# HGRN, second four heads: decay factors over three places, differences two levels ahead, one low part and the far scores elsewhere in the order

## The chip, the cores and the metric

The kernel runs on one core of one Trainium2 chip. The metric is device time in microseconds (us), lower is better. Times are shown for three runs of the kernel before, and for one profiled execution, whose trace gives every row below. In all of it, 256 tokens go through two transformer blocks; the change is in one sublayer, the HGRN mixer, sublayer 6 of 0 to 7.

## The reference, cut to what matters

The reference runs a first block (sparse attention with a convolution, then SwiGLU) and a second block of two layers (SwiGLU, differential attention, SwiGLU; then SwiGLU, HGRN, SwiGLU). The HGRN mixer is:

```python
def hgrn2(h, w_in, w_o, out_gain, lb):
    q, f, i, g = jnp.split(h @ w_in, [F, 2 * F, 2 * F + D_MODEL], axis=-1)
    log_forget = jnp.logaddexp(jnp.log(lb32), jnp.log1p(-lb32) + jax.nn.log_sigmoid(f32))
    k = (1.0 - lb32) * jax.nn.sigmoid(-f32)
    def step(state, inp):                    # chunks of 64 tokens
        G = jnp.cumsum(gc, axis=2)
        o_inter = jnp.einsum('bhtk,bhkv->bhtv', qc * jnp.exp(G), state)
        decay = jnp.exp(jnp.where(causal, G[:, :, :, None, :] - G[:, :, None, :, :], -jnp.inf))
        scores = jnp.einsum('bhtk,bhsk,bhtsk->bhts', qc, kc, decay)
        o_intra = jnp.einsum('bhts,bhsv->bhtv', scores, vc)
        ...
    o = rms_norm(o, out_gain.reshape(H, dv)) * jax.nn.silu(g)
    return o.reshape(B, S, D_MODEL) @ w_o
```

There are 8 heads with keys and values of 128, D_MODEL = 1024, S = 256. All is float32.

## The kernel before, in words

**Weights.** Every weight matrix streams through a ring of three slots in units of 128 x 2048 numbers. Sync's queue loads a unit (`raw`), ScalarE (ACT) rounds it to a high part (`hi(unit)`, whi, line 663), VectorE (DVE) takes the rest (`lo(unit)`, wlo, line 1250), and TensorE (PE) multiplies with both (three matmuls for one product, line 2062). The load of a unit waits for the low part of the unit three before it. In HGRN the units are U to U+19: U to U+15 for the input projection, U+16 to U+19 for the output product (`output_product`, called with `beside`, which puts other PE work between its parts). The output product goes over the units for the first 128 tokens, then for the others.

**The order** of all work is written out by hand, one list of calls for each engine; engines meet by semaphores only. On one engine nothing passes what stands ahead of it.

**HGRN on heads.** The heads are handled in two halves of four. For each half the scores of 256 tokens are made without the recurrence: level 0 is k times q on the diagonal, level L from 1 to 7 takes the pairs whose tokens lie in two neighbouring blocks of 64, 32, ... 1 tokens, level 8 the pairs between the first and the second 128 tokens, the "far" scores. For a half and a level:

- `differences(half, level)` (DVE, lines 1907 and 1909, for level 8 lines 1913 to 1916): G relative to the middle of each block pair, into a place that `decayed(level, half)` names.
- `exps(half, level)` (ACT, line 968, for level 8 lines 970 to 972): its exponential, in place.
- `decay(half, level)` (DVE, lines 1925 and 1928): times k and q, in place.
- `scores(half, level)` (PE, line 2507): 16 matmuls (8 for level 8) into bank 6 or 7 of PSUM by the level's parity; it waits for the decay and for the mask copy of the level before.
- `take_scores(half, level)` (DVE, lines 1937 and 1943): a masked copy of the product into the scores.

`step(half, level)` on DVE is the decay of a level, the differences of the next level, and the masked copy of the level before. `decayed` gives odd levels a place in `hf` and even levels one in `xn`, each with one half for heads 0 to 3 and one for heads 4 to 7. The differences of a level overwrite the place of two levels before, so from level 3 on they wait for the scores of that level (semaphore `lv_mm`, one count for each call of `scores`, nine for a half).

**Behind the levels** of the second half: `values(1, 0)` and `values(1, 1)` on PE (lines 2520 and 2522) multiply scores and values for the two token tiles, the second also with the far scores, which ACT copies (`take_far_scores(1)`, line 978). ACT squares the products (`square_last`, line 1017), DVE sums them (`sum_last`, lines 1964 and 1966) and multiplies product and gate (line 1969), GpSimd (POOL) takes the root (line 486), DVE scales (`norm_last`, line 1975), PE transposes (`turn_heads`, line 2177), DVE multiplies with the gain (`take_mixed`, line 1981), and ACT and DVE split it into high and low parts (lines 683 and 1303). Unit U+18's matmuls for the first tokens wait for that. ACT does the gate's silu (`silu_of(1)`, line 994) between `exps(1, 8)` and the squares. On PE `sum_columns(7)` (line 2070, 32 operations), the modulation sums for the next sublayer, stands between `values(1, 1)` and the turns.

Of the kernel before, what the change touches and what calls it, by code (L numbers as in the profile page):

```python
# [32 lines left out]
NT = TOK // P  # L33
# [25 lines left out]
LEVELS = (64, 32, 16, 8, 4, 2, 1)  # L59
# [90 lines left out]
def two_blocks(  # L150
# [30 lines left out]
    with ExitStack() as ctx:  # L181
        def sb(name, shape, dt=F32):
            return ctx.enter_context(nc.sbuf_tensor(name, shape, dt))

        def sem(name):
            return ctx.enter_context(nc.semaphore(name))
# [8 lines left out]
        xn = sb("xn", [P, NT, D])  # L195
        hf = sb("hf", [P, KT, TOK])
# [19 lines left out]
        half = st[:, 240:241]  # L216
# [25 lines left out]
        def by_head(flat):  # L242
            return flat.rearrange("p (h n) -> p h n", h=HEADS)
# [8 lines left out]
        def of_half(place, half):  # L252

            return place[:, HALF * half:HALF * (half + 1), :]

        def decayed(level, half):

            return of_half(hf if level % 2 else by_head(xn[:, :, :].rearrange("p t n -> p (t n)")), half)

        def halves(place, level):  # L260

# [62 lines left out]
        lv_mm, lv_copy, g_silu = sem("lv_mm"), sem("lv_copy"), sem("g_silu")  # L324
# [329 lines left out]
        def _(sc):  # L654
# [268 lines left out]
            def hgrn():  # L923

                U = FIRST[6]
# [49 lines left out]
                def take_far_scores(half):  # L975

                    sc.wait_ge(lv_mm, (len(LEVELS) + 2) * (half + 1))
                    sc.activation(far_scores(half), ps[:, 6, :].rearrange("p (h n) -> p h n", h=HALF), ACT.Copy).then_inc(lv_far, 1)
# [11 lines left out]
                def silu_of(half):  # L990

                    g = h_g[:, :, half * BANK:(half + 1) * BANK]
                    sc.wait_ge(vg_out, 6 + 2 * half)
                    sc.activation(g, g, ACT.Silu).then_inc(g_silu, 1)
# [19 lines left out]
                def square_last(t):  # L1014

                    sc.wait_ge(pv_mm, 4 + t + 1)
                    sc.activation(hf[:, HALF + 2 * t:HALF + 2 * t + 2, :], bank(h_bank(1, t)).rearrange("p (h n) -> p h n", h=2),
                                  ACT.Square).then_inc(head_sq, 1)
# [64 lines left out]
                exps(1, 7)  # L1083
                exps(1, 8)
                silu_of(1)
                square_last(0)
                take_far_scores(1)
                square_last(1)
                mixed_of(1, 0)
                mixed_of(1, 1)  # L1090
# [4 lines left out]
            for row, src in ((0, c), (8, c_2), (16, b_ada[0:1, 0:2 * D])):  # L1095
                n = src.shape[-1] // P
# [7 lines left out]
            U = FIRST[0]  # L1104
# [130 lines left out]
        def _(ve):  # L1235
# [10 lines left out]
            def lo(unit, lap=0, n=UNIT):  # L1246

                slot = unit % RING
                ve.wait_ge(w_hi, used(unit, lap))
                ve.tensor_tensor(wlo[:, slot, 0:n], raw[:, slot, 0:n], whi[:, slot, 0:n].bitcast(F32), ALU.subtract)\  # L1250
                    .then_inc(w_lo, 1)
# [249 lines left out]
            U = FIRST[0]  # L1501
# [355 lines left out]
            def hgrn():  # L1857

                U = FIRST[6]
# [36 lines left out]
                def differences(half, level):  # L1896

                    E, G = decayed(level, half), of_half(h_G, half)
                    if level >= 3:
                        ve.wait_ge(lv_mm, (len(LEVELS) + 2) * half + level - 1)  # L1900
                    if level == 1:
                        ve.wait_ge(k_ready, half + 1)
                    if level <= len(LEVELS):
                        n = LEVELS[level - 1]
                        e, g = halves(E, level), halves(G, level)
                        middle = g[:, :, 0, n - 1:n].to_broadcast((P, HALF * TOK // (2 * n), n))
                        done = ve.tensor_tensor(e[:, :, 0, :], middle, g[:, :, 0, :], ALU.subtract)
                        if level > 1:
                            done = ve.tensor_tensor(e[:, :, 1, :], g[:, :, 1, :], middle, ALU.subtract)
                    else:  # L1910
                        e, g = (a.rearrange("p h (c n) -> p h c n", n=CHUNK) for a in (E, G))
                        total = [g[:, :, c, CHUNK - 1:CHUNK].to_broadcast((P, HALF, CHUNK)) for c in range(3)]
                        link(ve.tensor_tensor(e[:, :, 0, :], total[0], g[:, :, 0, :], ALU.subtract))
                        ve.tensor_tensor(e[:, :, 0, :], e[:, :, 0, :], total[1], ALU.add)
                        ve.tensor_tensor(e[:, :, 1, :], total[1], g[:, :, 1, :], ALU.subtract)
                        done = ve.tensor_tensor(e[:, :, 3, :], g[:, :, 3, :], total[2], ALU.add)
                    done.then_inc(lv_sub, 1)
# [28 lines left out]
                def step(half, level):  # L1946

                    decay(half, level)
                    if level <= len(LEVELS):
                        differences(half, level + 1)  # L1950
                    take_scores(half, level - 1)

                def gate_heads(t):
# [6 lines left out]
                def sum_last(t):  # L1960

                    ve.wait_ge(head_sq, 6 + t + 1)
                    sums = st[:, 124 + 8 * t:128 + 8 * t]
                    link(ve.tensor_reduce(sums, hf[:, HALF + 2 * t:HALF + 2 * t + 2, :].rearrange("p a (h d) -> p (a h) d", h=2),
                                          axis=AX.X, op=ALU.add))
                    ve.tensor_scalar(sums, sums, 1.0 / P, EPS2, ALU.mult, ALU.add).then_inc(block_mean, 1)
                    if t == 0:
                        ve.wait_ge(g_silu, 2)
                    link(ve.tensor_tensor(h_o[:, 1, t, :], bank(h_bank(1, t)), h_g[:, t, BANK:D], ALU.mult))
# [45 lines left out]
                lo(U + 14)  # L2015
                differences(1, 1)
                step(0, 8)
                step(1, 1)
                lo(U + 15)
                step(1, 2)  # L2020
# [9 lines left out]
                lo(U + 17)  # L2030
                step(1, 5)
                step(1, 6)
                lo(U + 18)
                step(1, 7)
                step(1, 8)
                for t in range(NT):
                    sum_last(t)
                for t in range(NT):
                    norm_last(t)
                for t in range(NT):  # L2040
# [16 lines left out]
        def _(pe):  # L2057
# [407 lines left out]
            def hgrn():  # L2465

                U = FIRST[6]
# [13 lines left out]
                def scores(half, level):  # L2481

                    if level == 0:
                        pe.wait_ge(f_exp, half + 1)
                        pe.wait_ge(q_copied, half + 1)
                        if half:
                            pe.wait_ge(lv_copy, len(LEVELS) + 1)
                            pe.wait_ge(lv_far, 1)
                        else:
                            pe.wait_ge(gate_set, 7)  # L2490
                    else:
                        pe.wait_ge(lv_mul, (len(LEVELS) + 1) * half + level)
                        pe.wait_ge(lv_copy, (len(LEVELS) + 1) * half + max(level - 1, 1))
                    k, q, E = of_half(h_k, half), of_half(h_q, half), decayed(level, half)
                    for t in range(NT if level <= len(LEVELS) else 1):
                        cols = slice(t * P, (t + 1) * P)
                        for h in range(HALF):
                            dst = ps[:, 6 + t, h * P:(h + 1) * P]
                            if level == 0:
                                lhsT, rhs = k[:, h, cols], q[:, h, cols]  # L2500
                            elif level <= len(LEVELS):
                                g, n = t * HALF + h, LEVELS[level - 1]
                                lhsT, rhs = E[:, h, cols], later(E[:, h:h + 1, cols], level)[:, 0, :, :]
                                dst = level_bank(level)[:, g * P // 2:(g + 1) * P // 2].rearrange("p (b n) -> p b n", n=n)
                            else:
                                lhsT, rhs = E[:, h, 0:P], E[:, h, P:TOK]
                            done = pe.matmul(dst, lhsT, rhs, start=True, stop=True)  # L2507
                    done.then_inc(lv_mm, 1)
# [72 lines left out]
                def beside(j, t):  # L2581

                    if (j, t) == (0, 1):
                        scores(1, 4)
                    elif (j, t) == (1, 0):
                        scores(1, 5)
                    elif (j, t) == (2, 0):
                        scores(1, 6)
                        scores(1, 7)
                        values(1, 0)  # L2590
                        scores(1, 8)
                        values(1, 1)
                        sum_columns(7)
                        turn_heads(1, 0)
                        turn_heads(1, 1)
# [33 lines left out]
            U = FIRST[0]  # L2629
# [157 lines left out]
```

## Time and profile before

| | us |
|---|---|
| median of three runs | 1488.42 |
| lowest, highest | 1486.87, 1488.79 |
| profiled execution, its own time | 1488.98 |
| its span (first to last instruction) | 1487.30 |
| PE busy, DVE busy, ACT busy | 1409.5, 1060.7, 693.5 |
| mean granted clock of PE | 0.966 |

The granted clock is a share of full speed. Busy time counts an engine's own operations; in the timelines an operation's length is from its start to its end, and one behind it can start a little before that end. The bracket at the end of a row is the idle time ahead of it and what ended it. The HGRN stage's second half of heads lies at about 1209 to 1274 us of the span.

### The profile page before, as it was taken

The page shows a single profiled execution, that of the slowest core. Times are in us where ns is not written, and L with a number is a line of the kernel's source. Part 1 is how long each engine was busy: PE and PEld are TensorE (multiplying, and loading weights), DVE is VectorE, ACT ScalarE, POOL GpSimd, SP SyncE. Part 2 cuts the span into 40 slices and gives each one's busy share as a digit, 9 for nine tenths or more (in the row PEclk, how much of TensorE's full clock was granted, in tenths as well). Part 3 has the DMA queues.
Part 4 walks back from the last instruction along what each step waited for, and adds up shares of the span by engine and source line. Part 5 has one row for each costly group of instructions (what it writes and reads, how often), then busy time and mean ns, then how long its engine had stood idle before and what let it go on. Part 6 is the DMA issues. An engine that isn't in the chain of part 4 may idle for free.

```text
span 1487.3 us, 19356 instructions
## 1 busy us (share of the span) xinstructions
PE 1409.5 (95%) x6922; PEld 1176.2 (79%) x6922; DVE 1060.7 (71%) x1127; ACT 693.5 (47%) x897; POOL 186.2 (13%) x279
## 2 busy tenths in 40 slices
PE   5997899999799999999999999999999998899998
PEld 5896688888588887767788887888888987788887
DVE  5788877776678877685667775688866878655555
ACT  2463354433444345665643435444447764543442
POOL 3103211110301110221101102011101010000000
PEclk9995999999799999999999999999999998899999
DMA  9835379995389994533589973899945342256661
GB/s 355 301 143 212 129 260 313 309 315 186 129 279 345 373 378 146 187 113 114 169 274 312 309 270 108 296 337 343 349 142 170 114 142 85 95 188 214 229 226 66
DMA packets 187525, 335.61 MB, mean 226 GB/s; under 512 B 9169, under 2 KB 123453, under 8 KB 187216
## 3 DMA queue, kind: packets, MB, share of 16 engines
q1 hardware_dynamic: 160528, 237.95, 47.4%
q0 software_dynamic: 26736, 96.71, 18.1%
q8 instruction: 34, 0.56, 0.1%
q10 hardware_dynamic: 208, 0.23, 0.0%
q14 instruction: 19, 0.16, 0.0%
HBM read 332.23 MB, written 2.63 MB: 225 GB/s over the span
## 4 chain that ended last, share of the span: by engine, by line
PE 82%; DVE 8%; ACT 4%; POOL 2%; issue 2%; DMA 1%; SPq 0%; DVEq 0%; ACTq 0%; POOLq 0%
PE ps L2062 72%; DVE wlo L1250 2%; POOL st L486 2%; PE ps L2177 1%; PE ps L2246 1%; PE ps L2070 1%; PE ps L2507 1%; ACT whi L663 1%; DMA big<-in_w_ada 1%; ACT hf L671 1%; PE ps L2605 1%; ACT xn L696 1%; DVE xn L1312 1%; ACT xn L703 0%; PE ps L2191 0%
## 5 line engine op out<-in xcount | busy, mean ns | idle before, releaser
L1250 DVE TENSOR_TENSOR wlo<-raw,whi 128x2048 fp32r<-128x2048 f32 x206 | 470.2, 2285 | 151.5 <-ACT whi L663 150.4
L2062 PE MATMUL ps<-whi,hhi 128*128 128x512 f32 (+1 forms) x1208 | 494.9, 410 | 15.7 <-DVE hlo L1298 8.9
L663 ACT ACTIVATE whi<-raw 128x2048 fp32r<-128x2048 f32 x215 | 409.7, 1909 | 209.0 <-PE ps L2062 165.1
L2062 PE MATMUL ps<-whi,hlo 128*128 128x512 f32 (+1 forms) x1208 | 478.7, 396 | 0.0
L2062 PE MATMUL ps<-wlo,hhi 128*128 128x512 f32 (+1 forms) x1208 | 478.2, 396 | 0.0
L2062 PEld LDWEIGHTS ps<-whi,hhi 128*128 128x128 f32 x1208 | 232.3, 192 | 67.6 <-issue 11.9
L2062 PEld LDWEIGHTS ps<-whi,hlo 128*128 128x128 f32 x1208 | 231.6, 192 | 50.2
L2062 PEld LDWEIGHTS ps<-wlo,hhi 128*128 128x128 f32 x1208 | 232.5, 192 | 46.0 <-issue 1.9
L2062 PE MATMUL ps<-whi,ahi 128*128 128x512 f32 x400 | 156.1, 390 | 0.0
L2062 PE MATMUL ps<-whi,alo 128*128 128x512 f32 x400 | 155.7, 389 | 0.0
L2062 PE MATMUL ps<-wlo,ahi 128*128 128x512 f32 x400 | 155.7, 389 | 0.0
L1265 DVE SCALAR_TENSOR_TENSOR ada_acc<-ada_raw,csil,ada_acc 128x1024 f32<-128x1024 f32 x104 | 130.2, 1278 | 0.0
L519 POOL DMA_DIRECT2D ada_raw<-in_ada_w x96 | 50.9, 530 | 545.4 <-DVE ada_acc L1265 533.7
L747 ACT ACTIVATE act<-ps 128x256 f32<-128x256 f32 x110 | 41.9, 383 | 161.1 <-PE ps L2062 161.0
L751 ACT ACTIVATE ahi<-ps 128x512 fp32r<-128x512 f32 x50 | 29.9, 599 | 180.5 <-PE ps L2246 180.5
L1432 DVE TENSOR_TENSOR alo<-ps,ahi 128x512 fp32r<-128x512 f32 x50 | 34.5, 690 | 86.9 <-ACT ahi L751 86.9
L2062 PEld LDWEIGHTS ps<-whi,alo 128*128 128x128 f32 x400 | 75.1, 188 | 15.6
L2062 PEld LDWEIGHTS ps<-wlo,ahi 128*128 128x128 f32 x400 | 75.1, 188 | 15.4
L2062 PEld LDWEIGHTS ps<-whi,ahi 128*128 128x128 f32 x400 | 75.1, 188 | 15.4
L1427 DVE TENSOR_TENSOR act<-act,ps 128x256 f32<-128x256 f32 x110 | 42.9, 416 | 42.7 <-ACT act L747 42.6
L486 POOL TENSOR_TENSOR st<-st 128x1 f32<-128x1 f32 (+3 forms) x35 | 45.8, 1310 | 169.2 <-DVE st L1336 69.6
L2062 PE MATMUL ps<-hhi,whi 128*128 128x256 f32 x224 | 64.4, 287 | 1.2 <-DVE wlo L1250 1.2
(284 smaller groups left out, 1445.6 us busy)
## 6 DMA issues: line engine op xcount, KB each, us to landing
raw<-in_ffn_w_in SPq DMA_DIRECT2D x176, 512.0 KB
ada_raw<-in_ada_w POOLq DMA_DIRECT2D x96, 512.0 KB, 5.2
raw<-in_ffn_w_down SPq DMA_DIRECT2D x44, 1024.0 KB
big<-in_ada_w POOLq DMA_DIRECT2D x48, 512.0 KB, 6.2
raw<-in_hgrn_w_in SPq DMA_DIRECT2D x16, 1024.0 KB
raw<-in_attn_w_qkv SPq DMA_DIRECT2D x12, 1024.0 KB
ada_raw<-in_w_ada POOLq DMA_DIRECT2D x23, 512.0 KB, 4.9
raw<-in_w_gate SPq DMA_DIRECT2D x22, 512.0 KB
```

The costliest lines, as they stand in the source:

```text
L486: pool.tensor_tensor(cols, cols, half.to_broadcast((P, width)), ALU.pow).then_inc(signal, 1)
L519: pool.dma_start(ada_slot(p), w[bass.ds(kt * P, P), first + j * D:first + (j + 1) * D])\
L663: sc.activation(whi[:, slot, 0:n], raw[:, slot, 0:n], ACT.Copy).then_inc(w_hi, 1)
L671: done = sc.activation(hf[:, kt, toks], ps[:, 2 * t + 1, (kt - 4) * P:(kt - 3) * P], ACT.Identity, scale=modc[:, s % 2, 8 + kt:9 + kt], bi ...
L696: sc.activation(xn[:, t, cols], xs[:, t, cols], ACT.Square, scale=1.0 / 32, accum_out=st[:, part:part + 1]).then_inc(sums_s, 1)
L747: sc.activation(act[:, t, :], ps[:, 4 + t, 0:FC], ACT.Silu).then_inc(silu_done, 1)
L751: sc.activation(ahi.rearrange("p k n -> p (k n)"), bank(6), ACT.Copy).then_inc(ahi_ready, 1)
L1250: ve.tensor_tensor(wlo[:, slot, 0:n], raw[:, slot, 0:n], whi[:, slot, 0:n].bitcast(F32), ALU.subtract)\
L1265: ve.scalar_tensor_tensor(acc, ada_slot(p), csil[:, bass.ds((0 if a < 2 else 8) + kt, 1)], acc, ALU.mult, ALU.add).then_inc(a_used, 1)
L1427: ve.tensor_tensor(act[:, t, :], act[:, t, :], ps[:, 4 + t, FC:2 * FC], ALU.mult).then_inc(act_ready, 1)
L1432: ve.tensor_tensor(a_lo, bank(6), a_hi.bitcast(F32), ALU.subtract).then_inc(alo_ready, 1)
L2062: done = pe.matmul(dst, lhsT, rhs, start=first and n == 0, stop=final and n == 2, skip_group_check=True)
```

## The change

Three places instead of two hold the decay factors of the second half of heads: levels 1, 4, 7 in `hf`, heads 4 to 7; levels 2, 5, 8 in `xn`, heads 4 to 7; levels 3, 6 in `xn`, heads 0 to 3, which the first half of heads has left by then. On DVE, `step(1, level)` makes the differences of two levels ahead instead of one, up to level 8, and `differences(1, 2)` stands by itself after `step(0, 8)`. The waits follow: the differences of level 4 and on wait for the scores three levels before, those of level 3 for the last scores of the first half.

On DVE, `lo(U + 18)` goes from between `step(1, 6)` and `step(1, 7)` to between `sum_last(0)` and `sum_last(1)`. On PE, `scores(1, 8)` goes ahead of `values(1, 0)`. On ACT, `take_far_scores(1)` goes ahead of `square_last(0)`.

```diff
@@ -255,7 +255,12 @@
 
         def decayed(level, half):
 
-            return of_half(hf if level % 2 else by_head(xn[:, :, :].rearrange("p t n -> p (t n)")), half)
+            wide = by_head(xn[:, :, :].rearrange("p t n -> p (t n)"))
+            if half == 0:
+                return of_half(hf if level % 2 else wide, 0)
+            if level % 3 == 0:
+                return of_half(wide, 0)
+            return of_half(hf if level % 3 == 1 else wide, 1)
 
         def halves(place, level):
 
@@ -1083,8 +1088,8 @@
                 exps(1, 7)
                 exps(1, 8)
                 silu_of(1)
+                take_far_scores(1)
                 square_last(0)
-                take_far_scores(1)
                 square_last(1)
                 mixed_of(1, 0)
                 mixed_of(1, 1)
@@ -1896,8 +1901,10 @@
                 def differences(half, level):
 
                     E, G = decayed(level, half), of_half(h_G, half)
-                    if level >= 3:
-                        ve.wait_ge(lv_mm, (len(LEVELS) + 2) * half + level - 1)
+                    if level >= 3 + half:
+                        ve.wait_ge(lv_mm, (len(LEVELS) + 2) * half + level - 1 - half)
+                    if half and level == 3:
+                        ve.wait_ge(lv_mm, len(LEVELS) + 2)
                     if level == 1:
                         ve.wait_ge(k_ready, half + 1)
                     if level <= len(LEVELS):
@@ -1946,8 +1953,8 @@
                 def step(half, level):
 
                     decay(half, level)
-                    if level <= len(LEVELS):
-                        differences(half, level + 1)
+                    if level <= len(LEVELS) - half:
+                        differences(half, level + 1 + half)
                     take_scores(half, level - 1)
 
                 def gate_heads(t):
@@ -2015,6 +2022,7 @@
                 lo(U + 14)
                 differences(1, 1)
                 step(0, 8)
+                differences(1, 2)
                 step(1, 1)
                 lo(U + 15)
                 step(1, 2)
@@ -2030,11 +2038,11 @@
                 lo(U + 17)
                 step(1, 5)
                 step(1, 6)
-                lo(U + 18)
                 step(1, 7)
                 step(1, 8)
-                for t in range(NT):
-                    sum_last(t)
+                sum_last(0)
+                lo(U + 18)
+                sum_last(1)
                 for t in range(NT):
                     norm_last(t)
                 for t in range(NT):
@@ -2587,8 +2595,8 @@
                     elif (j, t) == (2, 0):
                         scores(1, 6)
                         scores(1, 7)
+                        scores(1, 8)
                         values(1, 0)
-                        scores(1, 8)
                         values(1, 1)
                         sum_columns(7)
                         turn_heads(1, 0)
```

## Rows read from the trace of the kernel before

**Rows 1.** The page: busy time, share of the span, instructions of PE; the chain by engine.

```profile
PE 1409.5 (95%) x6922; PEld 1176.2 (79%) x6922; DVE 1060.7 (71%) x1127; ACT 693.5 (47%) x897; POOL 186.2 (13%) x279
...
PE 82%; DVE 8%; ACT 4%; POOL 2%; issue 2%; DMA 1%; SPq 0%; DVEq 0%; ACTq 0%; POOLq 0%
```

**Rows 2.** The chain of waits, 1190 to 1320 us: start, us, engine, tile, line.

```profile
1258.35 2.07 PE ps L2520 x8
...
1266.60 3.83 PE ps L2070 x32
...
1273.30 14.51 PE ps L2062 x54
```

**Rows 3.** Timeline of VectorE (DVE), 1195 to 1330 us: start, us, then idle before.

```profile
1214.38 0.69 DVE L1925 TENSOR_TENSOR hf<-hf,big 128x512 f32<-128x512 f32 x1 [2.44 <-ACT hf L966]
...
1224.34 0.69 DVE L1925 TENSOR_TENSOR xn<-xn,big 128x512 f32<-128x512 f32 x1 [2.66 <-ACT xn L968]
...
1246.51 0.69 DVE L1925 TENSOR_TENSOR xn<-xn,big 128x512 f32<-128x512 f32 x1 [0.49 <-ACT xn L968]
...
1249.52 2.29 DVE L1250 TENSOR_TENSOR wlo<-raw,whi 128x2048 fp32r<-128x2048 f32 x1
1251.72 0.69 DVE L1925 TENSOR_TENSOR hf<-hf,big 128x512 f32<-128x512 f32 x1
...
1252.93 0.42 DVE L1913 TENSOR_TENSOR xn<-big 128x256 f32<-128x256 f32 x1
...
1254.40 1.30 DVE L1943 COPY_PREDICATED ada_acc<-mask,ps 128x512 f32<-128x512 uint8 x1
...
1257.00 1.29 DVE L1943 COPY_PREDICATED ada_acc<-mask,ps 128x512 f32<-128x512 uint8 x1
1261.09 0.69 DVE L1964 TENSOR_REDUCE st<-hf 128x4 f32<-128x512 f32 x1 [2.79 <-ACT hf L1017]
...
1267.34 0.69 DVE L1964 TENSOR_REDUCE st<-hf 128x4 f32<-128x512 f32 x1 [4.77 <-ACT hf L1017]
...
1268.85 1.29 DVE L1975 TENSOR_TENSOR big<-big,st 128x512 f32<-128x512 f32 x2
1271.10 0.69 DVE L1981 TENSOR_TENSOR hf<-ps,vec 128x512 f32<-128x512 f32 x1 [0.95 <-PE ps L2177]
...
1275.14 2.29 DVE L1250 TENSOR_TENSOR wlo<-raw,whi 128x2048 fp32r<-128x2048 f32 x1 [1.11 <-ACT whi L663]
```

**Rows 4.** Timeline of TensorE (PE), the same stretch.

```profile
1212.51 1.05 PE L2507 MATMUL ps<-xn 128*128 128x128 f32 x8
...
1217.92 1.28 PE L2520 MATMUL ps<-big,ada_acc 128*128 128x128 f32 x10
...
1244.23 2.00 PE L2507 MATMUL ps<-hf 128*128 128x64 f32 x16 [0.41 <-DVE hf L1928]
...
1248.87 1.89 PE L2507 MATMUL ps<-xn 128*128 128x64 f32 x16
1253.07 3.25 PE L2507 MATMUL ps<-hf 128*128 128x64 f32 x16 [2.30 <-DVE hf L1928]
```

**Rows 5.** Timeline of ScalarE (ACT), the same stretch.

```profile
1240.20 1.06 ACT L968 ACTIVATE hf<-hf 128x1024 f32<-128x1024 f32 x1 [0.76 <-DVE hf L1909]
...
1257.07 1.06 ACT L994 ACTIVATE big<-big 128x1024 f32<-128x1024 f32 x1
...
1273.21 1.89 ACT L663 ACTIVATE whi<-raw 128x2048 fp32r<-128x2048 f32 x1
```

**Rows 6.** Windows of 2 us: engines' busy time, then PE's granted clock, DMA share, GB/s.

```profile
1254.00:1256.00 2.00, 2.00 (x11) 2.00 (x10) 1.91 (x4) 1.47 (x4) 0.00 (x0) 0.50 1.00 327
...
1276.00:1278.00 2.00, 2.00 (x7) 1.61 (x6) 1.43 (x1) 0.00 (x0) 0.00 (x0) 0.63 0.00 0
```

**Rows 7.** Timeline of GpSimd (POOL), 610 to 621 us and 1252 to 1312 us.

```profile
610.90 3.61 POOL L486 TENSOR_TENSOR st<-st 128x8 f32<-128x8 f32 x1 [3.83 <-DVE st L1733]
...
1268.31 1.01 POOL L486 TENSOR_TENSOR st<-st 128x4 f32<-128x4 f32 x1 [5.24 <-DVE st L1966]
```

## The prediction

> **What bounds the kernel now.** I read the page first, then the chain of waits around the edited stage, then the three engines' timelines there, and last the granted clock. The page says TensorE (PE) is busy for 95% of the span and carries 82% of the chain that ends last [rows 1]; over the whole kernel PE is the bound, so an edit off PE pays only where PE stands idle waiting for it, or runs at the lower clock. The chain shows such a place: from 1258.35 us it goes through `values(1, 0)`, then the column sums (3.83 us), and reaches the first matmul of unit U+18 only at 1273.30 [rows 2]. Before that PE is late on VectorE (DVE): it idles 0.41 us ahead of `scores(1, 5)` and 2.30 us ahead of `scores(1, 7)`, each ended by the decay product [rows 4]. DVE is back to back over the same stretch except for 0.49 us [rows 3]. So from about 1246 to 1258 DVE's queue is the bound, after that a chain that goes PE, ACT, DVE, PE; while it runs PE's clock is granted at 0.50 (1.2 GHz), and it is back at full (2.4 GHz) only near 1277 [rows 6]. Every microsecond by which U+18 starts earlier should show at the end, as everything behind it (rest of the output product, last SwiGLU) is ordered by PE.
>
> **Part 1: order of differences, and the third place.** No instruction is added; the same differences are issued one step earlier, and the places let them. `differences(1, 2)` now stands after `step(0, 8)`. DVE idles 2.44 us there, ended by ACT's exponential of level 1 at 1214.38 [rows 3]; one pair costs 1.21 us (a pair of equal shape: from 1251.72 to 1252.93), so it is free: cover 2.44, need 1.21. If that cover were gone it costs 1.2 us, yet another 2.66 us idle stands at 1224.34 behind ACT, which would take it up [rows 3]. `step(1, 1)` now makes level 3 in the place half 0 had in xn; it waits for `scores(0, 8)`, whose 8 matmuls run from 1212.51 to 1213.56 [rows 4], before DVE gets there at 1215.6: no wait. From 1224.34 on each step still issues one pair, until the last: `step(1, 6)` makes level 8 instead of 7, and `step(1, 7)` none. The pair saved before the last mask copy is 1.2 us. The exponential of level 6 no longer follows its own differences: ACT waited 0.76 us for level 5 at 1240.20 [rows 5]; now levels 5 and 6 (1.06 each) can follow the 17th high part and end near 1241.5. So the 0.49 us idle at 1246.51 [rows 3] goes: DVE starts `decay(1, 6)` at 1246.0. New waits: level 8 waits for `scores(1, 5)`, which end at 1246.2 [rows 4], while DVE is there at 1247.2: nothing. Were it late, the exponential of level 8 and three DVE operations would queue behind it.
>
> **Part 2: lo(U+18) moved behind sum_last(0).** One operation of 2.20 us (1249.52 to 1251.72 [rows 3]) leaves the queue ahead of `decay(1, 7)`. Walk the queue: `decay(1, 6)` 1246.0 to 1247.2, differences of level 8 (four operations, 1252.93 to 1254.40, 1.47 us [rows 3]) to 1248.7, mask copy 0.6 to 1249.3, `decay(1, 7)` to 1250.5. Late next is PE: `scores(1, 6)` start at 1248.87 behind U+17's first token tile, whose start does not move (`decay(1, 5)` keeps its time), and end at 1250.8 [rows 4]; the mask copy of level 6 starts at 1250.9, 1.3 us, then `decay(1, 8)` 1.2, then the copy of level 7, 1.3 [rows 3]: end 1254.7 against 1258.3. ACT's exponential of level 8 is done near 1250, earlier than its decay. Gain here 3.6 us.
>
> **Part 3: scores(1, 8) ahead of values(1, 0), far scores ahead of the square.** The 8 matmuls of level 8 run from the end of `decay(1, 8)`, 1253.4, to 1254.5 at 1.05 us [rows 4], under the last mask copy. silu_of(1) (a table load, then 1.06 us [rows 5]) now ends near 1252.4, so ACT copies the far scores at once, by 1255.1, while `values(1, 0)` runs (1254.75 to 1255.8, ten such matmuls taking 1.28, or 0.11 from start to start [rows 4]). `values(1, 1)` follows with no wait: 16 more, to 1257.6. On DVE: 0.65 from the values' end to the first reduction (1260.42 to 1261.09 [rows 2, 3]) makes 1256.45, `sum_last(0)` takes 1.5 (as 1267.34 to 1268.85), and then lo(U+18), 2.2, is on the path now: 1260.15. Only then `sum_last(1)`, ready since 1258.3. It starts at 1260.15 against 1267.34 [rows 3].
>
> **The tail.** Before, from `sum_last(1)` to U+18's start it was 5.96 us, of which PE's column sums held the first turn until 1270.4 [rows 2]. Now these sums (at most 3.83) run 1257.6 to 1261.4 and hold nothing. `norm_last(0)` is done 2.2 us after `sum_last(1)` starts (it begins 1.51 after, 0.65 long [rows 3]), four transposes at the lower clock take 0.8, and from take_mixed to U+18 it was 2.20 (1271.10 to 1273.30): 5.2 us. U+18 starts at 1265.35, against 1273.30: 7.95 us earlier. Then nothing differs: U+18 has its low part (1260.15), and lo(U+19) was 1.8 us behind U+18's start (1275.14, ended by the high part that begins at 1273.21 [rows 3, 5]) and stays so; U+19's first tile starts 4.7 us behind U+18 while the clock is low for 3.9 us, as before. The load of U+21 is issued 8 us later but its high part is read only about 18 us on.
>
> At that point a rule bears on the new neighbours: GpSimd's root of sum 0 now runs beside lo(U+18). The trace has a root beside such a low part that took 3.61 us, against 1.01 beside the multiplications by roots, which themselves start with no idle time (1268.85) while the root of 1268.31 runs [rows 3, 7]. So a stretch of the root ends with lo(U+18) plus 1.0, 1261.15, and `norm_last(0)` is due at 1261.65: hidden. The Trainium skill (SBUF — State Buffer, Who interferes with whom) says that a VectorE operation with both inputs in SBUF and a GpSimd operation exclude each other, and whichever starts first holds the port. By it the root, first here (1257.4 to 1258.4), would hold lo(U+18) back some 0.6 us, and the gain would be 7.4, not 7.95; the multiplication at 1268.85 speaks against that.
>
> **Sum.** 3.6 (to the last mask copy) + 3.6 (from there to `sum_last(1)`, 9.05 us down to 5.45) + 0.75 (tail) = 7.95. The profiled execution took 1488.98 (span 1487.30): 1481.0 for it. It lies 0.56 above the median of the three runs, so I forecast 1480.5.
>
> **Rivals.**
> A: the clock falls among the last scores already, as in the execution shown (half at 1254 [rows 6]). For it: PE still waits 0.6 us ahead of `scores(1, 8)` and 0.25 after. Against: there it idled 2.30 us first. Price: `values(1, 0)` 1.9, `values(1, 1)` 3.6, column sums 3.9, all PE's, make 1254.7 into 1264.1, and the turn to U+18 is 3.0: 1267.1, gain 6.2, time 1482.2.
> B: the clock never falls, or is back when U+18 starts: 12 matmuls then end 1.9 us sooner, but lo(U+19) is ready only 4.1 us after U+18's start, so 0.6 more: gain 8.6, time 1479.8. Against: after the column sums PE idles about 1 us, and about 1.5 again after the turns.
> C: the places don't let the differences run ahead, because a score that they wait for is later than I read; then only lo(U+18) and the score order act. Without the saved pair and the 0.49 us, minus the 0.4 that PE's `scores(1, 6)` would have taken: gain 6.7, time 1481.7.
> D, the other side: PE's gaps, now shorter but more, leave it at half clock from about 1254 through the whole output product. A unit's first 12 matmuls cost 5.1 us at the low spacing (0.43) and 2.7 at the full one; three tiles of the first token and three of the second are 14 us more, less the 3.9 us low clock that were paid before (1.9 us), against the 8 gained (6.2 with A): 1494. It decides from the fifth of the six tiles at half clock on (8 + 1.9 over 2.4 us each). Against: at 1277 the clock came back within 4 us of dense matmuls [rows 6], and nothing thins them now.
> E: a stage behind has a bound of its own (a load, a bias), and takes the gain: 1487 to 1488.4. Against: PE's 54 matmuls in one piece from 1273.30 [rows 2].
>
> **How the numbers follow.** Chances: forecast 0.62, A 0.15, B 0.08, C 0.07, D 0.03, E 0.05. The range 1478.4 to 1484.0 takes in the forecast, A, B and C, with the spread of the runs (1.9 us) on either side of B and A. 0.2% (3 us) is about what measurement tells from no change: faster 0.92 (forecast, A, B, C), same 0.05, slower 0.03.
>
> **What would show it.** Right: no low part between `decay(1, 6)` and the last mask copy, which ends near 1254.7; `scores(1, 8)` before `values(1, 0)`; lo(U+18) between the two reductions; U+18's first matmul near 1265. Wrong: DVE idle ahead of a difference (C), a half clock at 1254 (A), values waiting for the far copy, lo(U+18) held back by a root, or U+19's first matmul waiting on its low part (B).

## The result, and the profile after

The changed kernel takes 1480.88 us (median of 9 runs, 1477.95 to 1486.58) against 1488.42 (9 runs, 1485.45 to 1489.90): ratio 0.995, 95% interval 0.9937 to 0.9963. So it is about 0.5% faster, and the interval excludes no change. The forecast was 1480.5, and the time lies in its range.

The profiled execution took 1478.56 with a span of 1476.9, 10.4 us less than the one before. Not all of that is the change. The start of `decay(1, 2)`, ahead of which all is the same in both kernels but one pair of differences in an idle gap, is 3.76 us earlier, 1220.58 against 1224.34 [rows 3]. So I count from that point:

| us from the start of decay(1, 2) | before | before, second trace | changed | changed, second trace |
|---|---|---|---|---|
| last mask copy ends | 33.9 | 33.9 | 30.1 | 30.1 |
| `sum_last(1)` starts | 43.0 | 41.2 | 37.0 | 36.9 |
| first matmul of U+18 | 49.0 | 46.6 | 42.65 | 42.3 |
| end of the span | 263.0 | 260.7 | 256.3 | 256.1 |

A count such as x8 is of recorded instructions. A float32 matmul of the code leaves two of them (5 fillers of a run below give x10), so a level's x16 is 8 matmuls and the x8 of level 8 is 4; the texts ahead call them 16 and 8.

Line numbers are 5 to 8 higher in the changed kernel (L1925 is L1932, L1943 is L1950, L2520 is L2528, L2070 is L2078, L2062 is L2070). On the page, PE is as busy a share of a shorter span, 10.6 us less busy time than in [rows 1]:

```profile
PE 1398.9 (95%) x6922; PEld 1166.8 (79%) x6922; DVE 1059.8 (72%) x1127; ACT 693.3 (47%) x897; POOL 185.5 (13%) x279
```

VectorE's timeline of the changed kernel, which answers to [rows 3]:

```profile
1220.58 0.69 DVE L1932 TENSOR_TENSOR xn<-xn,big 128x512 f32<-128x512 f32 x1 [2.67 <-ACT xn L973]
...
1242.14 0.69 DVE L1932 TENSOR_TENSOR xn<-xn,big 128x512 f32<-128x512 f32 x1
...
1247.07 1.32 DVE L1950 COPY_PREDICATED ada_acc<-mask,ps 128x512 f32<-128x512 uint8 x1 [0.37 <-PE ps L2515]
...
1249.41 1.29 DVE L1950 COPY_PREDICATED ada_acc<-mask,ps 128x512 f32<-128x512 uint8 x1
1253.90 0.69 DVE L1971 TENSOR_REDUCE st<-hf 128x4 f32<-128x512 f32 x1 [3.20 <-ACT hf L1022]
...
1255.41 2.29 DVE L1255 TENSOR_TENSOR wlo<-raw,whi 128x2048 fp32r<-128x2048 f32 x1
1257.62 0.68 DVE L1971 TENSOR_REDUCE st<-hf 128x4 f32<-128x512 f32 x1
...
1261.03 0.69 DVE L1988 TENSOR_TENSOR hf<-ps,vec 128x512 f32<-128x512 f32 x1 [0.61 <-PE ps L2185]
...
1265.07 2.29 DVE L1255 TENSOR_TENSOR wlo<-raw,whi 128x2048 fp32r<-128x2048 f32 x1 [1.11 <-ACT whi L668]
```

`decay(1, 6)` starts 21.56 us after `decay(1, 2)`, with no idle time ahead, against 22.17 before; there is no low part between it and the last mask copy; the copy of level 6 (1247.07) waits 0.37 us for PE's scores. The copy at 1249.41 is the last. Then DVE idles 3.20 us to the first sum, does lo(U+18) at 1255.41, and starts the second sum right behind it with no idle time: the low part is what it waits behind.

TensorE's timeline of the changed kernel, which answers to [rows 4]:

```profile
1246.87 1.95 PE L2515 MATMUL ps<-hf 128*128 128x64 f32 x16
1249.55 2.00 PE L2515 MATMUL ps<-xn 128*128 128x128 f32 x8 [0.73 <-DVE xn L1935]
1251.34 2.11 PE L2528 MATMUL ps<-big,ada_acc 128*128 128x128 f32 x10
...
1254.85 3.63 PE L2078 MATMUL ps<-ones,ada_acc 128*128 128x1 f32 x32
1259.88 1.97 PE L2185 MATMUL ps<-kc,big 128*128 128x128 f32 x8 [1.39 <-DVE big L1982]
1263.23 0.79 PE L2070 MATMUL ps<-whi,hhi 128*128 128x512 f32 x1 [1.38 <-DVE hlo L1308]
```

The 2.30 us idle ahead of `scores(1, 7)` is gone (1246.87, no bracket); 0.73 us stands ahead of `scores(1, 8)`, now before the values. But the 8 instructions of level 8 take 2.00 us, not 1.05, and the first ten of the values 2.11, not 1.28: half clock. The windows of 2 us (engines' busy time, granted clock, DMA share, GB/s) say when:

```profile
1250.00:1252.00 2.00, 2.00 (x12) 2.00 (x11) 0.70 (x1) 0.41 (x1) 0.00 (x0) 0.50 0.00 0
...
1256.00:1258.00 2.00, 2.00 (x20) 2.00 (x20) 2.00 (x2) 0.00 (x0) 0.00 (x0) 1.00 0.00 0
...
1264.00:1266.00 2.00, 2.00 (x7) 1.51 (x6) 0.93 (x1) 1.04 (x1) 0.00 (x0) 0.50 0.00 0
```

It is at 0.50 at 1250, at full at 1256, and at 0.50 again when U+18 starts. The kernel before has such a return too, and I had not read it: my prediction has the clock at half from 1254 until near 1277. Its window from 1268 to 1270 is at 1.00, under the column sums, most of which ran at full clock:

```profile
1266.39 4.03 PE L2070 MATMUL ps<-ones,ada_acc 128*128 128x1 f32 x32
```

```profile
1268.00:1270.00 2.00, 2.00 (x20) 2.00 (x19) 1.93 (x5) 0.00 (x0) 1.01 (x1) 1.00 0.00 0
```

ScalarE's rows, which answer to [rows 5], show the far copy (L983) ahead of both squares (L1022), and the silu long done:

```profile
1247.49 1.06 ACT L999 ACTIVATE big<-big 128x1024 f32<-128x1024 f32 x1
1251.59 0.60 ACT L983 ACTIVATE ada_acc<-ps 128x512 f32<-128x512 f32 x1 [3.04 <-PE ps L2515]
1253.27 0.60 ACT L1022 ACTIVATE hf<-ps 128x512 f32<-128x512 f32 x1 [1.08 <-PE ps L2528]
```

GpSimd's root of the first sum, beside lo(U+18):

```profile
1254.87 1.01 POOL L491 TENSOR_TENSOR st<-st 128x4 f32<-128x4 f32 x1 [34.41 <-DVE st L1973]
```

### The profile page after: what moved, and what is told of

Same layout as the page of the kernel before. It is cut to its first block, busy times and chain, and to the rows that moved or that the text cites. A ratio compares the mean times of both kernels' runs of the same rounds, so it can differ in the third digit from the quotient of the medians.

```text
span 1476.9 us, 19356 instructions
## 1 busy us (share of the span) xinstructions
PE 1398.9 (95%) x6922; PEld 1166.8 (79%) x6922; DVE 1059.8 (72%) x1127; ACT 693.3 (47%) x897; POOL 185.5 (13%) x279
## 4 chain that ended last, share of the span: by engine, by line
PE 78%; DVE 9%; ACT 5%; DMA 3%; issue 2%; POOL 2%; SPq 0%; DVEq 0%; ACTq 0%; POOLq 0%
PE ps L2070 69%; DVE wlo L1255 2%; DMA raw<-in_ffn_w_in 2%; PE ps L2185 2%; ACT whi L668 2%; POOL st L491 2%; PE ps L2515 1%; PE ps L2254 1%; PE ps L2078 1%; DMA big<-in_w_ada 1%; ACT hf L676 1%; ACT xn L701 1%; PE ps L2613 1%; DVE xn L1317 1%; ACT xn L708 0%
## 5 line engine op out<-in xcount | busy, mean ns | idle before, releaser
L2070 PE MATMUL ps<-whi,hhi 128*128 128x512 f32 (+1 forms) x1208 | 493.5, 409 | 16.6 <-DVE hlo L1303 8.9
L2070 PE MATMUL ps<-whi,hlo 128*128 128x512 f32 (+1 forms) x1208 | 477.3, 395 | 0.0
L2070 PE MATMUL ps<-wlo,hhi 128*128 128x512 f32 (+1 forms) x1208 | 476.2, 394 | 0.0
L2070 PEld LDWEIGHTS ps<-whi,hhi 128*128 128x128 f32 x1208 | 231.5, 192 | 68.2 <-issue 11.9
L2070 PEld LDWEIGHTS ps<-whi,hlo 128*128 128x128 f32 x1208 | 230.3, 191 | 50.0
L2070 PEld LDWEIGHTS ps<-wlo,hhi 128*128 128x128 f32 x1208 | 231.7, 192 | 45.7 <-issue 1.9
L2070 PE MATMUL ps<-whi,ahi 128*128 128x512 f32 x400 | 156.1, 390 | 0.0
L2070 PE MATMUL ps<-whi,alo 128*128 128x512 f32 x400 | 155.7, 389 | 0.0
L2070 PE MATMUL ps<-wlo,ahi 128*128 128x512 f32 x400 | 155.6, 389 | 0.0
L2070 PEld LDWEIGHTS ps<-whi,alo 128*128 128x128 f32 x400 | 75.1, 188 | 15.6
L2070 PEld LDWEIGHTS ps<-whi,ahi 128*128 128x128 f32 x400 | 75.1, 188 | 15.6 <-issue 0.2
L2070 PEld LDWEIGHTS ps<-wlo,ahi 128*128 128x128 f32 x400 | 75.1, 188 | 15.4
L1432 DVE TENSOR_TENSOR act<-act,ps 128x256 f32<-128x256 f32 x110 | 42.8, 415 | 41.8 <-ACT act L752 41.7
L2070 PE MATMUL ps<-hhi,whi 128*128 128x256 f32 x224 | 64.3, 287 | 1.2 <-DVE wlo L1255 1.2
```

The source lines that it names most:

```text
L1432: ve.tensor_tensor(act[:, t, :], act[:, t, :], ps[:, 4 + t, FC:2 * FC], ALU.mult).then_inc(act_ready, 1)
L2070: done = pe.matmul(dst, lhsT, rhs, start=first and n == 0, stop=final and n == 2, skip_group_check=True)
```

## The experiments

Lengths are from the start of `decay(1, 2)`, as in the table; "copy" is the end of the last mask copy. Every time is a median with the ratio to the kernel before, run beside it.

**The change taken apart.** First the differences alone: `decayed`, the waits, `step` and `differences(1, 2)` as in the change, nothing else.

> The kernel before with part 1 alone: three places and differences two levels ahead, differences(1, 2) after step(0, 8); lo(U+18) and the scores stay. I measure the stage from the start of decay(1, 2) on VectorE to the first matmul of U+18: 48.96 us before, 42.65 in the changed kernel. Theory (VectorE's queue): one pair of differences (1.2 us) and the wait of 0.49 for the exponential of level 6 leave the queue, so the stage is 1.7 to 1.9 shorter, 47.2; time about 1486.6. Rival (a score waited for is late and takes the place of the pair): 49.0, time 1488.4.

Measured: copy 31.8 (2.1 sooner), second sum 40.9, yet U+18 at 49.95; 1485.26 us, ratio 0.9965 (0.9952 to 0.9978). The queue's gain is there and the rival falls, but in this one trace it was lost on PE, after the second sum. Its column sums:

```profile
1266.26 6.83 PE L2078 MATMUL ps<-ones,ada_acc 128*128 128x1 f32 x32
```

The same 32 instructions took 4.03 before and 3.63 in the changed kernel. In this run the clock fell at 1257.1 and stayed at half for 23.9 us. To the end of the span it is 262.6, against 263.0 and 260.7 before: this one trace shows no gain at its end, the times do.

Then lo(U+18) alone:

```diff
-                lo(U + 18)
                 step(1, 7)
                 step(1, 8)
-                for t in range(NT):
-                    sum_last(t)
+                sum_last(0)
+                lo(U + 18)
+                sum_last(1)
```

> The kernel before with lo(U+18) alone moved between sum_last(0) and sum_last(1). Theory: 2.2 us leave the queue ahead of decay(1, 7), PE's scores(1, 6) give little of it back (level 8's differences wait for them), so the last mask copy ends about 2.1 us sooner; in its new place lo(U+18) is hidden, as the second sum is 9 us behind the copy there: stage 46.9, time about 1486.3. Rival (it only changes places on the path and costs its 2.2 us behind the first sum): 49.0, time 1488.4.

Measured: copy 32.4, U+18 47.4, end 261.1; 1483.81 us, ratio 0.9967 (0.9949 to 0.9984). The copy came 1.6 us sooner, not 2.1. U+18 stands between the two traces of before (49.0 and 46.6), so the stage does not decide between the theory and the rival; the times show a gain of 0.33%.

Then the far scores alone, `scores(1, 8)` ahead of `values(1, 0)` and the far copy ahead of the square:

> The kernel before with the order of level 8 alone changed: scores(1, 8) ahead of values(1, 0) on PE, the far copy ahead of the square on ScalarE. From decay(1, 2) on VectorE, the last mask copy still ends at 33.9 us. Theory (PE and ScalarE work leaves the chain behind that copy: level 8's matmuls 1.9 and the far copy 0.7 at half clock): stage 46 to 47 where the column sums meet the full clock, 3 us more where they meet half of it (the run of differences alone had 6.83 us for them against 3.63 to 4.03 elsewhere). Rival (the far scores were hidden anyway): 49.

Measured: copy 34.0, second sum 38.9, U+18 44.3, end 257.3; 1485.52 us, ratio 0.9971 (0.9953 to 0.999). More than the theory said, as PE came back to the full clock among the values:

```profile
1254.55 2.08 PE L2507 MATMUL ps<-xn 128*128 128x128 f32 x8 [0.72 <-DVE xn L1928]
1256.42 1.90 PE L2520 MATMUL ps<-big,ada_acc 128*128 128x128 f32 x10
...
1259.72 3.63 PE L2070 MATMUL ps<-ones,ada_acc 128*128 128x1 f32 x32
```

Level 8's 8 instructions take 2.08 us (half clock), the column sums 3.63 (full). In the trace this part alone gives 4.6 us at U+18 against the first trace of before, and 2.3 against the second.

The three parts alone gain 0.35, 0.33 and 0.29% in their times. Together that is 0.97%, more than the 0.5% of the whole change (0.64% in its second group of runs), so they hardly add up as if each were independent of the others. The three are not told apart by their times.

Parts 1 and 3 without part 2, lo(U+18) in its old place:

> The changed kernel with lo(U+18) back between step(1, 6) and step(1, 7), so parts 1 and 3 without part 2. Theory (in its new place between the two sums lo(U+18) gives back on the path what it saved in the queue): the last mask copy ends at 31.8 us instead of 30.1, but the second sum starts at about 35.5 instead of 37.0, and U+18 at 40.7 to 42.5 by the clock, no later than the 42.3 and 42.65 of the changed kernel. Rival (my prediction's sum, where part 2 is worth its 2.2 in the queue): about 44.5.

Measured: copy 31.85, second sum 36.9, U+18 42.4, end 255.3; 1482.0 us, ratio 0.9959 (0.9939 to 0.998). U+18 starts where it starts in the changed kernel (42.65, 42.3). So between the two sums the low part gives back what it saved in the queue: the copy is 1.7 us later without part 2, the second sum no later. It was not the 35.5 that I expected: level 8 and the first ten instructions of the values ran at half clock here too (2.08 and 2.04 us). The times (1482.0, and 1481.17 for the changed kernel in another group of runs) don't separate the two.

**The changed kernel and the kernel before once more.**

> The changed kernel once more. Theory: the profiled pair differs by 10.4 us of span, of which 3.8 stood before anything changed (opening, before 127 us), so that part does not repeat; the stage again takes 42 to 43.5 us, by where TensorE's clock falls, and the time is 1479 to 1483. Rival (the 3.8 us belong to the change): the first root of GpSimd again at 123.5 us and not near 127, time 1478.

> The kernel before once more, for its second trace. I measure also from the start of decay(1, 2) on VectorE to the end of the span: 263.0 us before, 256.3 and 256.1 in the two traces of the changed kernel. Theory (that length is the kernel's own, the rest of the 10.4 us between the first two traces came from ahead of the stage): 262 to 265 by where the clock falls, last mask copy again at 33.9. Rival (before varies there by as much as the gain): under 260.

The changed kernel again: 1481.17 us, ratio 0.9936 (0.9914 to 0.9957), the stage 42.3. Its first root came at 123.25, which by itself fits the rival; but the kernel before has 127.16 in one trace and 122.95 in the other, so the opening moves without the change. The end, 256.1 against 256.3, repeats. Over all traces of this study `decay(1, 2)` started between 1220.6 and 1227.1. The kernel before again: 1490.55, ratio to itself 1.0015 (0.9998 to 1.0032), which is about what the times resolve. Its length to the end is 260.7, below the 262 I expected: in the first trace `values(1, 1)` ran at half clock, in the second at full, with the column sums at 3.63.

```profile
1259.37 2.08 PE L2520 MATMUL ps<-big,ada_acc 128*128 128x128 f32 x8 [3.27 <-DVE ada_acc L1943]
...
1265.64 3.63 PE L2070 MATMUL ps<-ones,ada_acc 128*128 128x1 f32 x32
```

So the first trace's 9.05 us from the last copy to the second sum were 7.2 in the second. The far scores and the values were behind idle times of PE in both: 2.3 us ahead of `scores(1, 7)`, and ahead of the values 2.03 in the first trace, 3.27 in the second.

**lo(U+18) ahead of both sums.** In the changed kernel:

```diff
+                lo(U + 18)
                 sum_last(0)
-                lo(U + 18)
                 sum_last(1)
```

> The changed kernel with lo(U+18) ahead of sum_last(0) instead of behind it. Theory: VectorE idles 3.2 us there (1250.7 to 1253.9 in the changed kernel's trace), which covers 2.2; sum_last(1) then starts when its square is done, 1.9 us sooner, and the turns are held by the column sums, so U+18 starts 1.4 us sooner: stage 41.3, time 1.4 below the changed kernel, 1479.5. Rival (lo(U+18) is hidden where it stands, the tail is PE's own chain of values and column sums): stage unchanged at 42.6, same time.

> The changed kernel with lo(U+18) ahead of both sums, once more, beside the run with filled gaps. Theory: last mask copy at 30.1, second sum at 33.9 if the values run at full clock and up to 2.8 later at half; U+18 at 39.3 with the column sums at full clock, up to 5 us later where they meet the half clock. Rival (the first look's 39.3 is the queue's own figure and has no clock in it): 39.3 again whatever the clock.

Measured, first trace: second sum 33.9, U+18 39.3, end 252.1; 1479.39 us, ratio 0.993 (0.9909 to 0.9952). Second trace: 35.2, 40.6, 253.6; 1478.11, ratio 0.9932 (0.9907 to 0.9957). Both are shorter than the changed kernel's 256.1 and 256.3. The first gave more than the 1.4 us expected since its values ran at full clock; the second ran them at half and has 1.3 us more, so the rival (39.3 whatever the clock) falls. The second trace compares with the changed kernel at the same clock: its second sum is 1.8 to 1.9 us earlier and U+18 1.7 to 2.0. The times don't separate the two kernels: 1479.39 and 1481.17 in one group of runs, with intervals that overlap. VectorE in the first trace: the low part right behind the copy, then the sums, the second one waiting 0.24 us for its square.

```profile
1255.44 2.32 DVE L1255 TENSOR_TENSOR wlo<-raw,whi 128x2048 fp32r<-128x2048 f32 x1
1257.68 0.67 DVE L1971 TENSOR_REDUCE st<-hf 128x4 f32<-128x512 f32 x1
...
1259.38 0.69 DVE L1971 TENSOR_REDUCE st<-hf 128x4 f32<-128x512 f32 x1 [0.24 <-ACT hf L1022]
```

And PE there, level 8 in 1.16 us, the values' first ten in 1.38:

```profile
1254.49 1.16 PE L2515 MATMUL ps<-xn 128*128 128x128 f32 x8 [0.73 <-DVE xn L1935]
1255.70 1.38 PE L2528 MATMUL ps<-big,ada_acc 128*128 128x128 f32 x10
...
1264.84 0.79 PE L2070 MATMUL ps<-whi,hhi 128*128 128x512 f32 x1 [1.80 <-DVE hlo L1308]
```

**Without running ahead.** That kernel with the differences one level ahead in two places:

> The kernel with lo(U+18) ahead of both sums and the far scores first, but the differences one level ahead in two places, as before the change (parts 2 and 3 without part 1). Theory (the queue of VectorE sets the last mask copy): the copy ends at 32.4 as in the run of the low part alone, 2.2 later than the 30.1 with part 1; U+18 2.2 us later, 41.5 to 42.8; 254.5 to 256 us from decay(1, 2) to the end against 252.1 and 253.6. Rival (differences ahead are hidden once the low part is gone): 30.1 to 31 for the copy, and the same end.

Measured: copy 32.4, U+18 45.1, end 259.2; 1484.53 us, ratio 0.9968 (0.9953 to 0.9983). The copy is where the theory has it and the rival falls, but U+18 is 4.5 to 5.8 us later, not 2.2, and the end is beyond the 254.5 to 256 that I gave. `scores(1, 8)` have 2.07 us of idle ahead. The clock was at half from before them into the values, and it fell again within the column sums (4.81 us):

```profile
1254.39 2.08 PE L2507 MATMUL ps<-xn 128*128 128x128 f32 x8 [2.07 <-DVE xn L1928]
...
1260.30 4.81 PE L2070 MATMUL ps<-ones,ada_acc 128*128 128x1 f32 x32
```

**The clock itself.** PE's gaps filled, and ScalarE's high part of U+19 moved up:

```diff
+                        fill(4, 5)
                         scores(1, 8)
                         ...
                         turn_heads(1, 1)
+                        fill(5, 12)
```

`fill(b, n)` is n matmuls of the identity by ones into bank b, which nothing reads.

> As the kernel with lo(U+18) ahead of both sums, and PE's idle gaps filled with matmuls of the identity by ones into free banks: 5 ahead of scores(1, 8), 12 ahead of U+18; nothing reads them. Theory (the half clock comes from thin PE work there, and costs 1 to 5 us by where it falls): the clock stays at full through the values, the last mask copy at 30.1, U+18 at 39.3 to 40, its first 12 matmuls in 2.8 us instead of 4 to 5; time equal to the unfilled kernel or up to 1.5 us less. Rival (the single-column sums alone bring the clock down, whatever fills the gaps): the clock still falls within 5 us behind the column sums, and the time is the same or 0.5 us more, for the fillers.

> The kernel with lo(U+18) ahead of both sums, and ScalarE's hi(U+19) ahead of the far copy, where ScalarE idles 2.2 to 3.0 us (the high part takes 1.9). Theory: lo(U+19) starts 1.0 us sooner, but U+19's first matmul waits for it only where U+18's tile runs at full clock from its start, which no trace of the stage shows unless its gap is filled; so the stage and the time stay, at most 0.6 less. Rival (the high part comes into the way of the far copy or the square): U+18 up to 0.5 us later.

> The kernel with lo(U+18) ahead of both sums, hi(U+19) ahead of the far copy, 5 filling matmuls ahead of scores(1, 8) and 6 (not 12) ahead of U+18. With 12 they ran 1.6 us past the data, and took from the clock all of the stage's 10.2 us of half clock but 3.4. Theory (what is left of the clock's cost in the tail is U+18's tile at half clock, 2 us): U+18 at 39.3 to 39.7, its 12 first matmuls in 2.7 to 4 us, and 250.5 to 252 us from decay(1, 2) to the end against 252.1, 252.1 and 253.6 unfilled. Rival (6 are too few to bring the clock back before U+18): as unfilled, 252.1 to 253.6.

With 12 fillers: 1477.19 us, ratio 0.9917 (0.9893 to 0.9942); the values at full clock, half clock only for 3.4 us. It did fall within the column sums all the same, as the rival had it. And the fillers ran past their gap and U+18 started at 41.6, so my 39.3 to 40 was missed; end 253.5. The time is not told apart from the 1478.11 of the unfilled kernel beside it. hi(U+19) early alone: 1479.11 (0.9902 to 0.9958), lo(U+19) 1.2 us sooner, U+18 39.3 and end 252.1 as in the first trace without it: worth nothing there, as expected. Both, with 6 fillers ahead of U+18: 1475.41 us, ratio 0.9912 (0.9891 to 0.9933), U+18 40.3 (0.6 later than I said), its 12 first matmuls in 2.85 us, end 250.8, the least of all. PE of this kernel: fillers, level 8, fillers, U+18.

```profile
1254.31 1.33 PE L2592 MATMUL ps<-ones,kc 128*128 128x128 f32 x10
1255.48 1.06 PE L2515 MATMUL ps<-xn 128*128 128x128 f32 x8
...
1264.76 1.99 PE L2592 MATMUL ps<-ones,kc 128*128 128x128 f32 x12
1266.51 0.48 PE L2070 MATMUL ps<-whi,hhi 128*128 128x512 f32 x1
```

This version is faster than the kernel before. That it is faster than the changed kernel too is likely and not shown: its interval just fails to touch the first one of the changed kernel (0.9937 to 0.9963) and overlaps the second (0.9914 to 0.9957), and it has four runs, in a group of its own on another chip.

## Why the prediction was right, step by step

- **Part 1** held: no wait on the third place, `differences(1, 2)` in the idle gap, the wait at `decay(1, 6)` gone. Alone it brings the last copy 2.1 us forward (31.8 against 33.9).
- **The queue to the last mask copy** held best: I had 30.36 us from `decay(1, 2)` (1254.7), measured 30.1, with the predicted wait of 0.4 for `scores(1, 6)`.
- **Part 2** was costed rightly and not read to its end. The 1.8 to 2.2 us that it saves in the queue and the 1.85 by which `sum_last(1)` waits for it cancel, in my own numbers; the run without part 2 showed it (U+18 at 42.4 without, 42.3 and 42.65 with it). The idle 3.2 us one call earlier (it would have been 1.75 in my walk) takes the low part for nearly nothing.
- **Part 3** held in kind and is the largest at U+18 in the traces: 2.3 to 4.6 us alone, by which trace of before it stands against. In the times it is no larger than the others.
- **The clock among the values** is the step that failed in the profiled execution. I had level 8 and the values at full clock; they began at half, as rival A said. The squares came 1.2 us later, the second sum started at 37.0 instead of 35.8, and U+18 at 42.65 instead of 41.0. A's place, 42.8, was nearly met, and by luck: A kept the half clock through the column sums and priced them at 3.9, while the clock was back before them. At the half clock they take 6.83, and A's own sum would have come to 45.7. In five traces with 0.73 us idle ahead of `scores(1, 8)` and no fillers the clock fell there in three and not in two (the first trace with the low part ahead of both sums, and the one with the early high part); in all seven other traces without fillers, each with an idle time of 1.9 to 3.3 us between `scores(1, 6)` and the values, it fell. I gave A 0.15, too little.
- **The column sums** were mis-sized: "at most 3.83". I took that for their length at half clock, from a misread clock: it was back at full from about 1267.2 to 1270.6, under most of them. At half clock they are 6.83 (the run of the differences alone), and then the turns wait for them. Neither trace of the changed kernel has that, and none shows that it can't.
- **The tail** from the second sum to U+18: 5.2 predicted, 5.6 and 5.4 measured: take_mixed began 3.4 us behind the second sum (1257.62 to 1261.03), not 3.0.
- **The median** met the forecast more closely than the traces do. My 7.95 us came from one trace of before. Its 9.05 us from the last copy to `sum_last(1)` were 7.2 in the second, so 1.8 of the second 3.6 in my sum were that trace's half clock, and not the kernel's own. To the end of the span the traces give 4.4 to 6.8 us (two by two), the runs 5.5 to 9.4 (1488.42 times one less the ends of the interval). So that the median came within 0.4 us of the forecast is in part luck. That the kernel before meets the half clock at a worse place more often, as in the run with 6.83, would explain it; two traces don't show how often, and it stays open.
- **GpSimd and the low part**: the root started at 1254.87, lo(U+18) at 1255.41, at once behind the operation ahead of it, the root in 1.01 us: neither held the other. The Trainium skill (SBUF — State Buffer, Who interferes with whom) has an exclusive lock there and says that the order of issue decides who blocks. This pair does not agree with it: the root came first, and lo(U+18) behind it took 2.29 us, as always. The root that began behind a low part [rows 7] took 3.61, where one of the same 128 x 8 numbers took 1.63 at 631.64.

Rival C fell (the run of the differences alone), D and E too: nothing behind U+18 took the gain back. From its start to the end of the span it is 214.0 and 214.1 us in the traces of before, 213.7 and 213.8 in those of the changed kernel, and in the first of these the clock was back at full 3.5 us behind U+18's start. B's condition, a full clock at U+18, was in no trace without fillers. One bound of the range was set loosely: 1.9 us below B's 1479.8 is 1477.9, not 1478.4; the result does not touch it.

## What to carry to other kernels

Walk a moved operation to the next thing behind its new place, and look one call further for idle time: the same low part cost 1.8 to 1.9 us between two sums and nearly nothing ahead of them. Take the cost of a stretch from two traces of the kernel before, as one trace's clock can stand in it. Where PE idles ahead of small matmuls, price the stretch at both clock levels, single-column matmuls included, and give both a real chance. And compare two traces from a common event just ahead of the edit: here 3.8 of 10.4 us had nothing to do with it.

## What the runs showed that I had not expected

The 32 instructions of the column sums, with one moving column each, take 3.63 us at the full clock and 6.83 at half, so their length follows the clock though they move hardly any data. In thirteen of the fourteen traces the clock fell within them or in the 1.6 us behind them, with filled gaps as without; in the fourteenth it was at half already.

Fillers of 0.23 us each (5 matmuls in 1.2 us), put where PE idled 0.73, delayed `scores(1, 8)` by about 0.25 us. The clock stayed at full there in both runs that had them; but so it did in two of five without, so that the fillers did it is not shown. Ahead of U+18 the case is clearer: all twelve traces without fillers start U+18 at half clock, both with fillers (12 and 6) at full.
